# Local attention: q and z as separate products, z one tile later, and order tables per tile

## What is computed

```python
q, z = jnp.split(h @ w_in, 2, axis=-1)
q = rms_norm(q.reshape(B, T, B_Q_HEADS, B_HD), q_gain) * (B_HD ** -0.5)
logits = jnp.einsum("bnqkgd,bnskd->bnkgqs", q, k_band).astype(jnp.float32) + bias
m = jnp.maximum(jnp.max(logits, axis=-1, keepdims=True), sink)
p = jnp.exp(logits - m)
probs = p / (jnp.sum(p, axis=-1, keepdims=True) + jnp.exp(sink - m))
o = jnp.einsum("bnkgqs,bnskd->bnqkgd", probs.astype(v_band.dtype), v_band)
return (o.reshape(B, T, B_W) * jax.nn.silu(z)) @ w_out
```

## Time and profile before

| | before |
|---|---|
| median of 3 runs | 1616.17 us (1614.42 to 1616.56) |
| the profiled execution | 1615.91 us |
| its span in the trace | 1614.1 us, mean clock of PE 0.99 |
| busy PE, DVE, ACT, POOL | 1560.6, 883.5, 746.7, 241.8 us |
| local attention | 589 to 905 us of the span |

### The profile page before, as it was taken

The page is one execution under the profiler, slowest core; times in us unless marked ns, Lnnn a source line. Parts: engine busy times, 40 slices in busy tenths (PEclk is TensorE's granted clock), DMA queues, the critical chain, the costliest instruction groups (busy, mean ns, idle before and its releaser), DMA issues.

```text
span 1614.1 us, 20673 instructions
## 1 busy us (share of the span) xinstructions
PE 1560.6 (97%) x7686; PEld 1230.1 (76%) x7686; DVE 883.5 (55%) x1633; ACT 746.7 (46%) x1293; POOL 241.8 (15%) x451
## 2 busy tenths in 40 slices
PE   6899999999999999999998999999999999999998
PEld 5688888888878767777776887666677888888876
DVE  4766777776656445555555435444366343443466
ACT  4454455544553336665565324555545332332333
POOL 1043323343313002232222200000000000000000
PEclk9999999999999999999998999999999999999999
DMA  4221111111114332222221222111122323232321
GB/s 183 79 92 40 56 63 53 54 65 53 53 40 148 106 91 89 76 66 79 68 84 53 71 87 90 62 44 49 61 83 92 97 99 98 91 100 91 105 79 65
DMA packets 40163, 127.22 MB, mean 79 GB/s; under 512 B 4576, under 2 KB 9104, under 8 KB 40064
## 3 DMA queue, kind: packets, MB, share of 16 engines
q1 hardware_dynamic: 38112, 121.65, 23.3%
q0 software_dynamic: 1040, 3.27, 0.6%
q10 hardware_dynamic: 912, 0.99, 0.2%
HBM read 122.69 MB, written 2.15 MB: 77 GB/s over the span
## 4 chain that ended last, share of the span: by engine, by line
PE 80%; DVE 9%; ACT 7%; issue 3%; POOL 1%; DMA 1%; SPq 0%; ACTq 0%; DVEq 0%; POOLq 0%
PE ps L779 78%; ACT L L1659 3%; DVE wl L1852 2%; DVE qkv L1888 1%; DVE L L2337 1%; PE ps L1112 1%; ACT wh L1259 1%; PE ps L904 1%; DMA wraw<-in_wa 1%; DVE qb L1937 1%; POOL L L2621 1%; ACT L L1611 0%; DVE cin L1902 0%; DVE h L2466 0%; ACT qkv L1287 0%
## 5 line engine op out<-in xcount | busy, mean ns | idle before, releaser
L779 PE MATMUL ps<-xr,wh 128*128 128x512 f32 x2752 | 899.9, 408 | 15.0 <-DVE wl L1852 13.7
L779 PEld LDWEIGHTS ps<-xr,wh 128*128 128x128 f32 x2752 | 505.0, 190 | 145.0 <-issue 39.5
L779 PE MATMUL ps<-xr,wl 128*128 128x512 f32 x1376 | 542.4, 394 | 0.0
L1852 DVE TENSOR_TENSOR wl<-wraw,wh 128x1024 fp32r<-128x1024 f32 x214 | 262.5, 1233 | 156.1 <-ACT wh L1259 154.4
L779 PEld LDWEIGHTS ps<-xr,wl 128*128 128x128 f32 x1376 | 260.6, 189 | 57.4
L1259 ACT ACTIVATE wh<-wraw 128x1024 fp32r<-128x1024 f32 x214 | 222.4, 1049 | 83.4 <-PE ps L779 79.1
L779 PE MATMUL ps<-xm,wh 128*128 128x512 f32 x640 | 199.9, 394 | 6.7 <-DVE xm L2451 3.7
L779 PEld LDWEIGHTS ps<-xm,wh 128*128 128x128 f32 x640 | 120.2, 189 | 35.3 <-DVE xm L2451 5.0
L2621 POOL TENSOR_SCALAR L<-L,m 128x256 f32<-128x256 f32 (+1 forms) x128 | 80.8, 653 | 315.3 <-DVE m L2352 315.3
L779 PE MATMUL ps<-xm,wl 128*128 128x512 f32 x320 | 125.3, 392 | 0.0
L1888 DVE SCALAR_TENSOR_TENSOR qkv<-cin,gains,qkv 128x512 f32<-128x512 f32 x96 | 83.4, 869 | 11.1 <-ACT qkv L1287 10.3
(11 more groups left out here) (258 smaller groups left out, 1776.7 us busy)
## 6 DMA issues: line engine op xcount, KB each, us to landing
wraw<-in_wa SPq DMA_DIRECT2D x48, 512.0 KB, 3.7
wraw<-in_wb SPq DMA_DIRECT2D x32, 512.0 KB, 3.9
wraw<-in_wu SPq DMA_DIRECT2D x32, 512.0 KB, 3.6
wraw<-in_wd SPq DMA_DIRECT2D x32, 512.0 KB, 3.7
wraw<-in_wao SPq DMA_DIRECT2D x16, 512.0 KB, 3.7
wraw<-in_wbo SPq DMA_DIRECT2D x16, 512.0 KB, 3.9
wraw<-in_wc SPq DMA_DIRECT2D x16, 512.0 KB, 3.7
bias<-rel_rows SPq DMA_DIRECT2D x16, 256.0 KB, 4.1
```

The costliest lines, as they stand in the source:

```text
L779: return e.matmul(out, w, x, start=start, stop=stop, skip_group_check=True)
L1852: e.tensor_tensor(m.wl[:, i % N_SPLIT, :], m.raw[:, i % N_RAW, :], m.wh[:, i % N_SPLIT, :].bitcast(F), ALU.subtract).then_inc(s.wlo, 1)
```

## The change

The products of q and z become groups of their own (`qb`, `zb`). Tile 0's z comes after q(0)'s head sum and not before; z of a tile comes in the tile before its own, and q two tiles before: beside tile j stand z(j+1), then q(j+2) and its `qnorm`. The weight blocks are loaded in that order. Four tables say how the steps lie: `b-` for tile 0's logits, `b` for tiles 0 to 13, `b14` (z(15) and the first output pieces) and `b15`. `x` is no part: it only takes product steps. Silu of two tiles moves to the odd tile, and so do the two gating products on VectorE: that of tile j-1 stands after the first copy and the drain of z, that of tile j at the end.

```diff
@@ -78,8 +78,9 @@
     out = [b for i in sorted(PRODUCTS) for what, h in PRODUCTS[i] for g in groups_of(what, h) for b in g]
     out += [("wao", b) for b in beside(3)]
     out += [("wkv", b) for b in range(4)]
-    for j in range(16):
-        out += [("wb", j), ("wb", 16 + j)]
+    out += [("wb", 0), ("wb", 16), ("wb", 1)]
+    for j in range(15):
+        out += [("wb", 17 + j)] + ([("wb", j + 2)] if j < 14 else [])
     out += [("wbo", b) for b in beside(2)]
     for j in range(4):
         out += [("wc", 15 - j)] if j else []
@@ -267,6 +268,10 @@
     "a8": plan("p0 q1 p2 q3 q1 q0 p0 q0 p3 q0 p0 q0 p0 q0 p1 r1 r0 r1 r0 p0 r0 p2 p0 r0 p0 r0 p2 r5 p0 r1 p0 r2 r1"),
     "a9": plan("q1 q5 q2 q5 q3 q1 q3 q2 r9 r1 r3 r0 r1 r0 r2 r0 r4 r2 r4"),
     "a": plan("p0 q2 q0 p4 q2 q0 p1 p1 q4 q0 p0 q1 p0 q1 p0 r2 r2 r0 p1 r0 p3 p1 r0 p2 r0 r1 r2 r3 p1 r2 p0 p2 r16"),
+    "b-": plan("x4 a3 a0 a0 a0 a4 a4 a3 a0 a0"),
+    "b": plan("x5 b0 a0 a6 b0 b0 a0 a0 b0 b3 a2 a0 a1 a1 b0 a0 b0 b0 a0 b0 b0"),
+    "b14": plan("b2 x2 a0 b1 a0 b0 a0 a0 b0 a1 b5 b2 a2 b1 b0 a2 b7 a0 a6"),
+    "b15": plan("x2 b1 b4 b4 b4 b0 b0 b0 b2 b0"),
 }
 STEPS = {"gates": 3, "prep": 14, "levels": 8, "recur": 11, "kv_post": 4, "attend": 9, "attend2": 9, "split_o": 1, "split_ob": 1,
          "stick0": 12, "stick1": 14, "ple": 8, "post": 8}
@@ -358,22 +363,30 @@
     do("bias", 0)
     do("bias", 1)
 
-    def qz(j):
-        return gemm("qz", [[("wb", j)], [("wb", 16 + j)]], 0, j)
-
-    def tiles(j):
-        yield from qz(j)
+    def q_normed(j):
+        yield from gemm("qb", [[("wb", j)]], 0, j)
         do("qnorm", j)
 
-    merge(qz(0), 2, part("kv_post"))
-    do("qnorm", 0)
-    merge(tiles(1), 2, part("attend", 0))
+    def beside_attention(j):
+        if j < 15:
+            yield from gemm("zb", [[("wb", 17 + j)]], 0, j + 1)
+        if j < 14:
+            yield from q_normed(j + 2)
+
+    merge(q_normed(0), 2, part("kv_post"))
+    g = chain(gemm("zb", [[("wb", 16)]], 0, 0), q_normed(1))
+    weave(g, PLAN["b-"], {"a": part("attend", 0)}, None)
+    drain(g)
     out = gemm("bo", pair_groups("wbo", 8), 2, None, 0)
-
     for j in range(16):
-        side = tiles(j + 2) if j < 14 else pieces_out("split_ob", out, 2, 0, *((0, 8) if j == 14 else (8, 14)))
-        merge(side, 0.85 if j < 14 else 1.4 if j == 14 else 2, part("attend2", j),
-              part("attend", j + 1) if j < 15 else None, lead=4)
+        g = beside_attention(j)
+        if j >= 14:
+            g = chain(g, pieces_out("split_ob", out, 2, 0, *((0, 8) if j == 14 else (8, 14))))
+        parts = {"b": part("attend2", j)}
+        if j < 15:
+            parts["a"] = part("attend", j + 1)
+        weave(g, PLAN.get(f"b{j}", PLAN["b"]), parts, None)
+        drain(g)
     drain(split_pieces("split_ob", 14, 16))
     banks((4, 5, 6, 7, 0, 1))
     drain(out)
...
@@ -795,7 +808,7 @@
             e.wait_ge(s.olo, k + 1)
         elif name == "kv":
             e.wait_ge(s.slo, k + 1)
-        elif name == "qz" and a == 0:
+        elif name == "qb" and a == 0:
             e.wait_ge(s.slo, 8 + k + 1)
         elif name == "bo":
             e.wait_ge(s.oblo, k + 1)
@@ -821,8 +834,10 @@
             return [(s.h[0], n + 1)]
         if name == "kv":
             return [(s.kv, n + 1)]
-        if name == "qz":
-            return [((s.q, s.z)[n], a + 1)]
+        if name == "qb":
+            return [(s.q, a + 1)]
+        if name == "zb":
+            return [(s.z, a + 1)]
         if name == "bo":
             return [(s.h[1], n + 1)]
         if name == "qkv":
...
@@ -1665,8 +1680,8 @@
 
     @part
     def attend2(j):
-        if j % 2 == 0:
-            for jj in (j, j + 1):
+        if j % 2:
+            for jj in (j - 1, j):
                 e.wait_ge(s.z, jj + 1)
                 e.activation(m.XF[:, 16 + jj, :], m.XF[:, 16 + jj, :], ACT.Silu).then_inc(s.zs, 1)
             tables()
@@ -1927,17 +1942,18 @@
     def falling(v):
         return bass.AP(v.tensor, v.offset + 127, [list(v.ap[0]), [128, 4], [-1, 128]])
 
-    def evac_qz(n, bank, i, j):
+    def evac_qb(n, bank, i, j):
         e.wait_ge(s.wused, i + 1)
-        if n == 0:
-            if j < 2:
-                e.wait_ge(s.vt_p, j + 1)
-            if j >= 3:
-                e.wait_ge(s.lg_p, 8 * (j - 3) + 8)
-            e.tensor_tensor(falling(m.qb[:, j % 3, :]), m.bk_of(bank), m.rb[:].rearrange("p (n c) -> p n c", n=4),
-                            ALU.mult).then_inc(s.q, 1)
-        else:
-            e.tensor_tensor(m.XF[:, 16 + j, :], bank[:], m.rb[:], ALU.mult).then_inc(s.z, 1)
+        if j < 2:
+            e.wait_ge(s.vt_p, j + 1)
+        if j >= 3:
+            e.wait_ge(s.lg_p, 8 * (j - 3) + 8)
+        e.tensor_tensor(falling(m.qb[:, j % 3, :]), m.bk_of(bank), m.rb[:].rearrange("p (n c) -> p n c", n=4),
+                        ALU.mult).then_inc(s.q, 1)
+
+    def evac_zb(n, bank, i, j):
+        e.wait_ge(s.wused, i + 1)
+        e.tensor_tensor(m.XF[:, 16 + j, :], bank[:], m.rb[:], ALU.mult).then_inc(s.z, 1)
 
     def evac_qkv(n, bank, i, j):
         par = j % 2
...
@@ -2354,6 +2370,11 @@
 
     @part
     def attend2(j):
+        def gated(j):
+            e.wait_ge(s.pv_p, 4 * j + 4)
+            e.wait_ge(s.zs, j + 1)
+            e.tensor_tensor(m.XF[:, 16 + j, :], m.banks[6 + j % 2][:], m.XF[:, 16 + j, :], ALU.mult).then_inc(s.ob, 1)
+
         for n in range(4):
             b = turned()
             if n % 2 == 0:
@@ -2362,11 +2383,12 @@
                 if j:
                     e.wait_ge(s.pv_p, 4 * (j - 1) + n + 1)
                 e.tensor_copy(m.pT[:, n, k0:], m.bk(b)[:, k0:]).then_inc(s.pT_v, 1)
+            elif n == 1 and j % 2:
+                gated(j - 1)
             yield
         yield from idle(4)
-        e.wait_ge(s.pv_p, 4 * j + 4)
-        e.wait_ge(s.zs, j + 1)
-        e.tensor_tensor(m.XF[:, 16 + j, :], m.banks[6 + j % 2][:], m.XF[:, 16 + j, :], ALU.mult).then_inc(s.ob, 1)
+        if j % 2:
+            gated(j)
         yield
 
     @part
```

More of the change, by code:

```diff
@@ L611, in pieces @@
             return [(x[:, 16 + k, :], x[:, 24 + k, :]) for k in range(8)]
-        if key in ("qz", "qkv", "pool"):
+        if key in ("qb", "zb", "qkv", "pool"):
             return [(x[:, k, :], x[:, 8 + k, :]) for k in range(8)]
@@ L1584, in scale @@
         key = ("kv_norm", "b_norm", "g_mix_pre")[at]
-        X = m.pieces(("kv", "qz", "qkv")[at])
+        X = m.pieces(("kv", "qb", "qkv")[at])
         e.wait_ge(s.wused, (BLOCK["wao", 15], BLOCK["wao", 15], BLOCK["wbo", 15])[at] + 1)
@@ L2035, in evac_gate @@
         e.tensor_tensor(g, g, m.H[:, n, :], ALU.add).then_inc(s.go, 1)
-    EVAC = {"head": evac_head, "z": evac_z, "ao": evac_ao, "bo": evac_bo, "kv": evac_kv, "qz": evac_qz,
+    EVAC = {"head": evac_head, "z": evac_z, "ao": evac_ao, "bo": evac_bo, "kv": evac_kv, "qb": evac_qb, "zb": evac_zb,
             "qkv": evac_qkv, "pool": evac_pool, "mix": evac_mix, "up": evac_up, "down": evac_down, "gate": evac_gate}
```

## The result

The changed kernel takes 1599.47 us (median of 4 runs, 1598.86 to 1600.34) against 1615.30 for the kernel before on the same chips (4 runs): ratio 0.9903, interval 0.9886 to 0.9921. That is 15.8 us less. 1603.3 was forecast, 12.9 less than the 1616.17 that the kernel before had then. The profiled execution took 1599.54 us with a span of 1597.7, 16.4 less than before.

What follows compares the result with a forecast made beforehand. PE, busy 97% of the span, was taken as the bound, leaving only idle and low-clock time to win. Terms -3.5 (steady tiles), +1.8 (start), -11.2 (end) summed to -12.9, from 1616.17 to 1603.3 us; range 1598 to 1610.

Steps and rivals of the forecast that it cites:

- Steady tiles: Local attention, 14 tiles: period 18.09 to 17.84 us (10.09 to logits B, then 7.75), -3.5 us; bounds 0 and 5.9.
- that floor at 17.67: Steady tiles: PE's own work alone needs 17.67 us a tile, 0.17 under the predicted period set by the chain.
- One sign named for a wrong forecast: Steady tiles: PE still waiting 0.3 us per tile on L1611, the square of q, would show the chain account wrong.
- Start: Tile 0 and before: stalls of 2.4 and 1.7 us before two head sums; +1.8 us, bounds +0.1 and +3.5.
- The fall of the clock that I charged: Start: PE's clock falls after the 2.4 us stall, costing 1.7 us.
- rival (a): Start: clock holds after the first stall, everything else as forecast; -14.6 us, 1601.6 us; chance 0.18.
- End: Tiles 14 and 15: new order and z(15)'s pieces recover lost PE time; -11.2 us, bounds 12.1 and 6.
- where I charged 0.9: Tile 15: about 0.5 us waiting for POOL's scaling before tr3 and 0.4 for the copy n=2 before values.
- Rival (b): Steady tiles gain nothing, VectorE later or the second L pair as long as now; -9.4 us, 1606.8 us; chance 0.14.
- (c): End stalls again, POOL or VectorE's queue late, and the clock falls; 5 us more, 1608.3 us; chance 0.13.
- (d): Odd tiles: a silu burst 2.8 us longer delays the weight split and VectorE; 16.5 us more, 1619.8 us; chance 0.04.
- (e): No measurable effect: Rival (b), (c) and clock falls at both start stalls together; -2.7 us, 1613.5 us; chance 0.06.

Runs made afterwards that it cites:

- Experiment 1: Kernel before with only the new order table `b` for tiles 0 to 13 added: 1611.92 us, ratio 0.9978.
- 8: Also called shift1: changed kernel with one product piece in table `b` moved from ahead of logits B to behind them: 1595.49 us, ratio 0.9885.
- after_again: The changed kernel itself, unaltered, timed again on a second chip: 1600.11 us, ratio 0.9914.
- shift1_gate: Changed kernel with the moved piece of 8, and the even tile's gating moved to the odd tile's end: 1595.16 us, ratio 0.9885.
- nocover: Changed kernel with z(15) multiplied in tile 13 as before the change, with tables to fit: 1605.05 us, ratio 0.9946.
- regroup_rate: Changed kernel without table `b`; tiles 0 to 13 go by the old fixed rate: 1621.59 us, ratio 1.0039.
- Experiments 2: Kernel before with the new order of tiles 14 and 15, silu and gating in pairs, z(15) still in tile 13: 1609.07 us, ratio 0.9958.
- 3: Kernel before with all new tables, silu and gating in pairs, q and z still grouped together: 1605.09 us, ratio 0.9935.
- 4: Kernel before with only silu and gating of two tiles moved in pairs to the odd tile: 1610.67 us, ratio 0.9978.
- 6: The run nocover: changed kernel with z(15) multiplied in tile 13, after q(15), and tables to fit: 1605.05 us, ratio 0.9946.
- start2: Changed kernel with q(0)'s end between kv_post's head sums, z(0) pieces before q(0)'s head sum, q(1) opened before logits B: 1598.01 us, ratio 0.9899.

## Why the prediction was right

The time lay in the range, 3.8 us below the forecast; as a gain, 15.8 us came for 12.9. The profiled executions, by which the terms can be told apart, differ by 16.4:

- **Steady tiles**, forecast -3.5: (856.00-606.87)/14 = 17.795 us, so 14 x 0.29 = -4.1. Both parts of the period came out within 0.06 us. Experiment 1 shows that the table alone does it; 8 shows that the chain set the period, since moving a single piece brought it down to PE's own work, 17.49. The forecast had that floor at 17.67, too high by 0.18, so its bound of 5.9 us for this term was none: 14 x 0.60 is 8.4. One sign named for a wrong forecast came too, a wait for L1611 (now L1626) of nearly 0.3 a tile. The sign was ill chosen. The profile showed 0.26 before and shows 0.26 now, but before, the idle stretch was 648.47-(647.83+0.23) = 0.41 with a gap of 0.1 ahead of logits B besides, and now it is what the chain has over PE's work, about 0.3. The period and the 1.95 us from L to exps tell it, the wait does not.
- **Start**, forecast +1.8: +0.2. Before, q(1)'s head sum ended at 613.2; now it ended at 607.8, and z(1)'s 5.5 us come after it; another 0.1 is what the changed kernel was ahead when the stage began. The stalls were 2.3 and 1.5 us for 2.4 and 1.7. The fall of the clock that I charged did not come in this execution; this is rival (a), 0.18, and its sum of -14.6 is nearer. It did come in four of the six profiled kernels that share this start (after_again, shift1, shift1_gate and nocover; not in the changed kernel's first trace nor in regroup_rate). So the forecast had the stalls, and whether a fall follows them differs from one execution to the next: that this term came out small in the profiled one is luck.
- **End**, forecast -11.2: -12.4. From the head sum's end (856.94) to the end of tile 15's values (888.54) are 31.6 us with 33 pieces, against 37.8 with 24: 6.2 us less, and nine pieces more of 0.69. That is 0.3 beyond the bound of 12.1. No stall came where I charged 0.9: POOL took 4.49 us in tile 15 where I feared 8.40 again, and the copy n=2, begun at 885.95, was done before the values at 886.87. Experiments 2, 3, 4 and 6 divide it, added in this order: silu and gating moved, 3.9 (4.9 in the traces); the order of L, exps and splits on top of that, 2.8 (2.2); z(15) as cover, about 5. The forecast had the cover and the order, but put nothing on silu's move, which alone gives a third of the gain at the end.
- The remaining difference, 0.1 us, lies before the stage.

Rival (b) is refuted by the period of 17.80, (c) by the end's full clock and the want of a wait there, (d) by the equal length of odd and even tiles, and (e) falls with (b) and (c). Behind the table load silu again started at once (load at 876.78, 1.28 us long, silu at 878.07). The Trainium skill, ScalarE: Activation LUTs, What ACT_TABLE_LOAD costs, gives about 1380 ns more for a drain at each switch; this trace does not show it.

## What to carry to other kernels

When PE is busy for nearly all of a stage and a small wait repeats, follow what the waiting step needs back to the last product that feeds it, and move drains and splits out of that stretch: 1.6 us of VectorE work between two operations cost 0.3 us a tile here, and a drain and a split one step too early in the start's table brought a stall of 2.1 us. Keep independent products for the ends of a pipeline, where its chain lies bare, and never put the product whose result is needed next last in its turn without other work behind it. After such a change count pieces before and after the hand-over again: one more moved was worth 4.6 us.

## What the hardware did that I had not expected

The same instructions with the same stall do not always lose PE's clock. Of six traces with the 2.3 us stall at the start, four show it at half (1.2 GHz) for about 3.4 us afterwards and two do not. All five traces with the 2.5 us wait of the old start show such a fall. The fall at the start cost 1.6 us (17.51 against 15.92 above).

A fall need not cost anything. A wait of 1.9 us that ends between 1182 and 1209 us, which all fourteen traces have, is followed by a fall in eight and not in six. In the six, a wait of 1.2 us for VectorE follows 10 us later, as here in `start2`; in the eight it is missing:

```profile
1185.09 0.73 PE L797 MATMUL ps<-xm,wh 128*128 128x512 f32 x2 [1.93 <-DVE xm L2480]
...
1195.10 0.72 PE L797 MATMUL ps<-xm,wh 128*128 128x512 f32 x2 [1.24 <-DVE xm L2480]
```

From the end of the 1.9 us wait to the end of the span all fourteen traces take 411.1 to 411.5 us, with a fall or without. PE at half clock only used up time in which it would have waited for VectorE.

POOL's eight scaling operations took 4.86 us in a steady tile before and 3.89 after. In tile 15 they took 8.40 before, 5.42 with silu moved alone and 4.49 beside the output splits of the new order. The same operations take a time that changes with the order of the steps; what makes the difference was not separated.
